# A one-layer hybrid encoder step: last output tile in halves, third norm's rows earlier, attention's filler pieces laid out anew

## The chip, the core and the metric

The kernel runs on one core of a Trainium2 chip. The metric is the device time of one execution in microseconds (us). A core has five engines that run side by side and meet at semaphores: PE (matrix products, with its weight loads listed as PEld), DVE (vector), ACT (activations), POOL (general) and SP (here it only issues DMAs).

## The reference

576 token rows (512 of a prompt, 64 of a sample that also sees 256 cached positions) go through one layer, width 1024. With h = RMSNorm(x), one projection feeds 8 heads of forgetting attention (FoX: causal, with sums of log forget gates added to the logits) and 8 heads of latent attention (MLA: low-rank queries and keys, a rotary part). Their two outputs are normalised, joined and projected (`w_o`); then comes a 4-head attention to 256 memory rows, then the feed-forward block of hidden width 2816, and a final norm:

```
x = x + mixed @ w_o
x = x + o @ w_mo                                   # o: attention of RMSNorm(x) to the memory
hf = rms_norm(x, g_ffn)                            # the third norm
x = x + (silu(hf @ w_gate) * (hf @ w_up)) @ w_down
y = rms_norm(x, g_final)
```

New keys, values, gates and latents are outputs too. All is float32.

## The kernel before, in words

**Layout.** Channels lie on the 128 partitions and the 576 tokens in the free dimension, in 8 channel tiles; `x_low` and `x_high` are the token halves 0:288 and 288:576. A float32 product is made of three products of parts: each operand is split into a high part (ACT) and a low rest (POOL or DVE), and `product` (L450 to L454) issues high x high, low x high, high x low. PSUM has eight banks; "pair p" is banks 2p and 2p+1, a token half in each.

**Weights** come in blocks: SP loads one, ACT makes the high part (`split`), POOL the low part (`rest`).

**Queries and keys of FoX.** Before the attention loop PE computes queries and keys of head pairs 0 and 1 as four whole blocks (`full`, the loop behind the value projection). DVE writes them to `qt` and `kt`; `query_dup` and `key_dup` (DVE), `query_hi` and `key_hi` (ACT), `query_lo` and `key_lo` (POOL) make the parts that the scores use. Pairs 2 and 3 are computed inside the loop.

**The attention loop** runs over ticks `s`. Tick s belongs to head s//5 and query tile s%5 (FoX heads are ticks 0 to 39, MLA heads 40 to 79). In a tick PE computes the scores of tick s, one *filler* chunk, and the transposes of tick s-2; at s%5 == 3 also `values` of an earlier head. DVE takes the maxima and evicts the last filler and half of the transposes, ACT takes the exponentials and the other half. Scores of tick s wait for the exponential of tick s-2. Filler chunks sit at ticks written out by hand: `QK_AT` (queries and keys of FoX, one token half, 24 matmuls), `UQ_AT` (MLA queries), `KP_AT` and `V_AT` (MLA keys, values), `RB_AT` (the reciprocals of a head pair's sums, spread over rows; POOL builds its source `rb` at `RB_BUILD`), `FC_AT` and `FR_AT` (norm of the FoX output: column sums, then rows; ACT takes a square root two ticks behind `FC_AT`), `WO_AT` (first half of `w_o`). `HIGH_AT`, `LOW_AT`, `REST_AT`, `SPLIT_AT`, `KR_AT` and the tables of `query_*`, `key_*` say at which tick ACT, DVE and POOL do the rest. The finished output of FoX head pair 0 first goes to a tile of its own, `olof0`, and is copied by DVE to `olof` behind tick 18 (L1712, semaphore `s_omove`), since `olof` shares its place with the low part of h; POOL's first `rb` waits for that copy.

**The third norm and the first gate and up blocks.** PE computes the gate and up products of the first two hidden tiles in full (blocks c = 0 to 3, 48 matmuls each), with column sums for the norm behind c = 0 (`columns`, L470) and the row spread (`spread`, L478) behind c = 2. The other 20 hidden tiles use seven half-size products (`seven`) of sums of weights (`weight_sums`, `op_rest`, `op_high`, `op_low`) and sums of inputs (`t_sum`, `t_high`, `t_rest`). DVE's order is: the four `t_sum`, the norm's rows, gate of tile 0, `weight_sums` of the first step, and so on; the seventh product of a step waits for DVE's `gate_low` of the step behind it (L1938).

**The end.** The down projection has 8 output tiles in three blocks each; in every block PE does both token halves. DVE multiplies by the norm's rows (L2010), adds to x (L2012), ACT squares, DVE adds to `sqacc` (L2017). Behind the last tile come column sums (L470), a square root (ACT), a reciprocal (L2019), the row spread (L478), eight multiplications of 576 columns (L2022), and eight stores.

Of the kernel before, what the change touches and what calls it, by code (L numbers as in the profile page):

```python
# [14 lines left out]
D = 1024  # L15
TP, TS = 512, 64
T = TP + TS
# [46 lines left out]
def nth(tick):  # L64
# [4 lines left out]
FILLER_END = {15: QK_AT[1], 16: QK_AT[3], 17: QK_AT[5], 18: QK_AT[7], 19: UQ_AT[1] + 1, 20: V_AT[0][6], 21: UQ_AT[3] + 1, 22: UQ_AT[5] + 1, 23: V_AT[1][6],  # L69
# [9 lines left out]
    0, 1, 6, 11, 21, 31, 36, (56, 80), 66, 71, 76, 78)  # L79

# [6 lines left out]
def build(nc, i_, o_, cum_dram):  # L87
# [38 lines left out]
    olof0, _ = place("olof0", [128, T], F32, c)  # L126
# [37 lines left out]
    vbase = c  # L164
    va, _ = place("va", [128, 2, 7, 4, 64], F32, vbase + 14336)
# [55 lines left out]
    with ExitStack() as ctx:  # L221
# [36 lines left out]
        s_init, s_mask, s_zero, s_omove = sem("s_init"), sem("s_mask"), sem("s_zero"), sem("s_omove")  # L258
# [40 lines left out]
        s_y, s_yst = sem("s_y"), sem("s_yst")  # L299
# [132 lines left out]

        def half_a(c):

            return slice(64 * (c % 2), 64 * (c % 2) + 64)
# [11 lines left out]
        def _(pe):  # L447
# [100 lines left out]
            for i in range(4):  # L548
                if i == 0:
                    pe.wait_ge(s_kvn, 2)  # L550
                else:
                    pe.wait_ge(s_vev, (2, 4, 5)[i - 1])
                full(B_QK + i, PAIR_QK[i])
# [53 lines left out]
            def values(c):  # L607
# [3 lines left out]
                if c == 0:  # L611
                    pe.wait_ge(s_vhi, 7)
                    pe.wait_ge(s_qkev, 4)
# [23 lines left out]
            def head_part(i, bank, k0):  # L637

                b, half = B_QK + 4 + i // 2, i % 2
# [6 lines left out]
            def filler(s):  # L646
                if s + 1 in QK_AT:
                    i = QK_AT.index(s + 1)
                    bank = filler_bank(nth(s + 1))
                    pe.wait_ge(f_lo, B_QK + 4 + i // 2 + 1)  # L650
# [71 lines left out]
            for s in range(LAST):  # L722
# [7 lines left out]
                if s == 84:  # L730
# [3 lines left out]
                elif s == 86:  # L734
# [3 lines left out]
                elif s == 89:  # L738
                    pe.wait_ge(n_rc, 2)
                    spread(ps[:, 5, :], small[:, S_MRC:S_MRC + 2], range(2)).then_inc(n_row, 1)  # L740
                elif s == 90:
                    memory_keys(1)
                elif s == 92:
# [3 lines left out]
                elif s == 94:  # L747
# [160 lines left out]
            for c in range(4):  # L908
                pe.wait_ge(g_lo, c + 1)
                pe.wait_ge(r_x, 8 + (5, 6, 8, 7)[c])  # L910
                wide(c, KT, lambda k: [ffw(c, lo, KT, 128)[:, k, :] for lo in (0, 1)], x1,
                     wait_k=(lambda k: pe.wait_ge(r_lo, 8 + k + 1)) if c == 0 else None).then_inc(g_used, 1)
                if c == 0:
                    pe.wait_ge(r_acc, 7 + 7)
                    pe.wait_ge(r_x, 8 + 7)
                    columns(7, sqacc, at=HT).then_inc(n_col, 1)
                if c == 2:
                    pe.wait_ge(n_rc, 5)
# [1604 lines left out]
```

## Time and profile before

| | us |
|---|---|
| runs (3) | 893.72, 894.79, 897.13; median 894.79 |
| the profiled execution | 897.35, of which the span is 895.6 |
| PE busy | 848.6, 95% of the span |
| DVE, ACT, POOL busy | 551.0, 400.5, 365.5 |
| mean granted PE clock | 0.982 of full speed |
| DMA | 75.49 MB, mean 84 GB/s |

PE has two granted clock levels, 1.2 GHz (0.50 in the rows) and 2.4 GHz (1.00). Since PE is nearly always busy, time can only come from the stretches in which it waits, from those at the lower clock, and from the end, where nothing is left for it.

### The profile page before, as it was taken

The page shows a single profiled execution, that of the slowest core. Times are in us where ns is not written, and L with a number is a line of the kernel's source. Part 1 is how long each engine was busy: PE and PEld are TensorE (multiplying, and loading weights), DVE is VectorE, ACT ScalarE, POOL GpSimd, SP SyncE. Part 2 cuts the span into 40 slices and gives each one's busy share as a digit, 9 for nine tenths or more (in the row PEclk, how much of TensorE's full clock was granted, in tenths as well). Part 3 has the DMA queues.
Part 4 walks back from the last instruction along what each step waited for, and adds up shares of the span by engine and source line. Part 5 has one row for each costly group of instructions (what it writes and reads, how often), then busy time and mean ns, then how long its engine had stood idle before and what let it go on. Part 6 is the DMA issues. An engine that isn't in the chain of part 4 may idle for free.

```text
span 895.6 us, 16042 instructions
## 1 busy us (share of the span) xinstructions
PE 848.6 (95%) x5930; PEld 784.8 (88%) x5930; DVE 551.0 (62%) x875; ACT 400.5 (45%) x736; POOL 365.5 (41%) x212
## 2 busy tenths in 40 slices
PE   6999999899999899989899989999999999999994
PEld 6988988677887799978589989999999998999994
DVE  5256354656555854863546899999999989312213
ACT  6443454535556533444535455555555555222110
POOL 2644854634422544662129233333333335433410
PEclk9999999999999999999999999999999999999997
DMA  7332421100105323333012212222222233223102
GB/s 244 109 111 69 156 80 44 56 1 19 48 1 172 113 65 91 120 112 97 0 45 98 94 49 94 94 94 93 94 94 94 93 127 90 87 85 89 42 1 106
DMA packets 25239, 75.49 MB, mean 84 GB/s; under 512 B 2896, under 2 KB 5272, under 8 KB 25048
## 3 DMA queue, kind: packets, MB, share of 16 engines
q1 hardware_dynamic: 25184, 74.74, 26.2%
q8 instruction: 37, 0.61, 0.3%
q14 instruction: 18, 0.15, 0.1%
HBM read 68.20 MB, written 6.53 MB: 83 GB/s over the span
## 4 chain that ended last, share of the span: by engine, by line
PE 71%; DVE 6%; issue 3%; ACT 1%; POOL 0%; DVEq 0%; ACTq 0%
PE ps L452 21%; PE ps L453 20%; PE ps L454 20%; PE ps L619 3%; PE ps L603 1%; PE ps L855 1%; PE ps L470 1%; PE ps L478 1%; DVE xb L2022 1%; DVE hlo L1753 1%; DVE tl L1863 1%; PE ps L625 0%; PE ps L588 0%; PE ps L582 0%; DVE sqacc L1760 0%
## 5 line engine op out<-in xcount | busy, mean ns | idle before, releaser
L452 PE MATMUL ps<-hhi,whi 128*128 128x288 f32 x896 | 270.0, 301 | 18.8 <-DVE hlo L1455 6.6
L453 PE MATMUL ps<-hhi,wlo 128*128 128x288 f32 x896 | 266.1, 297 | 0.0
L454 PE MATMUL ps<-hlo,whi 128*128 128x288 f32 x800 | 237.8, 297 | 0.0
L2033 POOL TENSOR_TENSOR wlo<-wraw,whi 128x1024 fp32r<-128x1024 f32 (+1 forms) x48 | 115.3, 2407 | 212.2 <-ACT whi L980 203.1
L452 PEld LDWEIGHTS ps<-hhi,whi 128*128 128x128 f32 x896 | 170.3, 190 | 22.2 <-issue 10.5
L980 ACT ACTIVATE whi<-wraw 128x1024 fp32r<-128x1024 f32 (+3 forms) x138 | 114.8, 838 | 137.3 <-PE ps L454 119.8
L453 PEld LDWEIGHTS ps<-hhi,wlo 128*128 128x128 f32 x896 | 169.9, 190 | 0.1
L454 PEld LDWEIGHTS ps<-hlo,whi 128*128 128x128 f32 x800 | 151.5, 189 | 0.0
L2179 POOL TENSOR_TENSOR wlo<-wraw,whi 128x512 fp32r<-128x512 f32 x60 | 77.3, 1302 | 155.2 <-ACT whi L980 155.2
L454 PE MATMUL ps<-hidlo,whi 128*128 128x288 f32 x352 | 103.9, 295 | 0.0
L2193 POOL TENSOR_TENSOR wlo<-wraw,whi 128x1024 fp32r<-128x1024 f32 (+1 forms) x24 | 56.8, 2372 | 77.6 <-ACT whi L980 77.6
L1606 DVE TENSOR_REDUCE small<-ps 128x1 f32<-128x128 f32 (+4 forms) x80 | 39.0, 488 | 75.6 <-PE ps L588 54.5
L454 PE MATMUL ps<-tl,whi 128*128 128x288 f32 x240 | 71.4, 297 | 0.0
L452 PE MATMUL ps<-th,whi 128*128 128x288 f32 x240 | 71.0, 296 | 0.4 <-DVE wlo L1909 0.4
L453 PE MATMUL ps<-th,wlo 128*128 128x288 f32 x240 | 71.3, 297 | 0.0
L980 ACT ACTIVATE whi<-ss 128x512 fp32r<-128x512 f32 x61 | 38.4, 632 | 65.3 <-PE ps L454 37.5
L454 PEld LDWEIGHTS ps<-hidlo,whi 128*128 128x128 f32 x352 | 66.1, 188 | 0.0
L980 ACT ACTIVATE probs<-ps,small 128x128 f32<-128x128 f32 (+4 forms) x80 | 41.9, 524 | 49.4 <-DVE small L1606 48.8
L2010 DVE TENSOR_TENSOR tmp<-ps,rstd 128x576 f32<-128x576 f32 x8 | 6.1, 758 | 88.8 <-PE ps L454 88.8
L452 PE MATMUL ps<-hidhi,whi 128*128 128x288 f32 x192 | 56.8, 296 | 2.1 <-DVE hidlo L1992 2.1
L453 PE MATMUL ps<-hidhi,wlo 128*128 128x288 f32 x192 | 56.8, 296 | 0.0
L452 PEld LDWEIGHTS ps<-th,whi 128*128 128x128 f32 x240 | 45.2, 188 | 0.6 <-DVE wlo L1909 0.6
(277 smaller groups left out, 1870.8 us busy)
## 6 DMA issues: line engine op xcount, KB each, us to landing
wraw<-w_ff SPq DMA_DIRECT2D x44, 512.0 KB, 4.1
wraw<-w_front SPq DMA_DIRECT2D x41, 512.0 KB, 3.6
wraw<-w_down SPq DMA_DIRECT2D x16, 512.0 KB, 3.6
wraw<-w_down SPq DMA_DIRECT2D x8, 384.0 KB, 3.3
wraw<-w_front SPq DMA_DIRECT2D x7, 384.0 KB, 3.6
xs<-x_t SPq DMA_DIRECT2D x8, 288.0 KB, 6.1
xa<-x_t SPq DMA_DIRECT2D x8, 288.0 KB, 5.1
out_y<-xb SPq DMA_DIRECT2D x8, 288.0 KB, 2.3
```

What stands on the lines that cost most here:

```text
L452: nc.tensor.matmul(out, lh, rh, start=start, stop=False)
L453: nc.tensor.matmul(out, ll, rh, start=False, stop=False)
L454: return nc.tensor.matmul(out, lh, rl, start=False, stop=stop)
L470: mm = nc.tensor.matmul(ps[:, bank, at + tt:at + tt + 1], source[:, 128 * tt:128 * tt + 128], ones[:, 0:1], start=True, stop=True)
L478: mm = nc.tensor.transpose(out[:, at:at + n], col[0:n, tt:tt + 1].to_broadcast([n, 128]), ident[0:n, 0:n])
L603: mm = nc.tensor.transpose(ps[:, 2 + s % 2, 128 * kb:128 * kb + n], probs[0:n, P_AT[u] + 128 * kb:P_AT[u] + 128 * kb + 128], ident[0:n, 0:n])
L619: mm = nc.tensor.matmul(ps[0:64, 4, 128 * kb:512], va[:, g, kb, h, :], pt[:, 512 * kb:512 * kb + 512 - 128 * kb], start=kb == 0, stop=kb == 3)
L980: return nc.scalar.activation(out, src, func, **kw)
L1606: v.tensor_reduce(nmax, ps[0:n, s % 2, 0:w], AX, ALU.max, negate=True).then_inc(s_mx, 1)
L2033: g.tensor_tensor(wlo[:, b % 3, 0:n], wraw[:, b % 2, 0:n], f(whi[:, b % 3, 0:n]), ALU.subtract).then_inc(f_lo, 1)
L2179: g.tensor_tensor(w_operand(1, j), src, f(w_operand(0, j)), ALU.subtract).then_inc(g_lo, 1)
L2193: g.tensor_tensor(ffw(n, 1, 1, w)[:, 0, :], (wraw2, wraw)[n % 4 // 2][:, n % 2, 0:w], f(ffw(n, 0, 1, w)[:, 0, :]), ALU.subtract).then_inc( ...
```

## The change: what it does

Three parts. (1) The last output tile of the down projection is computed one token half after the other. Column sums, square root, reciprocal and rows of the final norm are made for each half by itself, in tiles of 96 tokens, those of the first half between the products of the second; outputs are written and stored in halves (16 stores). A square root without use is put ahead, at tile 6. (2) The third norm's rows are spread in the middle of block c = 1; DVE does the first step's `weight_sums` and the gate of tile 0 ahead of all four `t_sum`; ACT and DVE orders follow; PE waits for DVE's copy of the rows (`n_rs`) ahead of c = 2. (3) The key block of FoX pair 1 moves from ahead of the loop into ticks 1 and 3; all filler ticks are laid out anew, with one tick more; FoX outputs get a tile `fo` of their own, so the copy and `s_omove` go.

```diff
-LAST = 95
-QK_AT = (1, 3, 5, 7, 12, 14, 16, 18)
-UQ_AT = (24, 34, 43, 45, 49, 56, 60, 69)
-KP_AT = (30, 40, 51, 62)
-V_AT = ((28, 29, 32, 33, 38, 39, 42), (54, 55, 58, 59, 64, 65, 66))
-RB_AT = (22, 26, 36, 47, 67, 73, 79, 85)
-FC_AT = 53
-FR_AT = 71
-WO_AT = (75, 77, 81, 83, 87, 89, 91, 93)
+LAST = 96
+QK_AT = (1, 3, 5, 7, 10, 12, 15, 17, 20, 22)
+UQ_AT = (25, 34, 36, 46, 50, 56, 64, 70)
+KP_AT = (30, 40, 54, 60)
+V_AT = ((27, 32, 33, 42, 43, 44, 45), (52, 53, 58, 59, 62, 63, 66))
+RB_AT = (23, 28, 38, 48, 68, 74, 78, 86)
+FC_AT = 67
+FR_AT = 72
+WO_AT = (76, 80, 82, 84, 88, 90, 92, 94)
...
-            for i in range(4):
+            for i in range(3):
...
                 full(B_QK + i, PAIR_QK[i])
...
+                if c == 2:
+                    pe.wait_ge(n_rs, 5)
+                for k in range(KT):
+                    if c == 0:
+                        pe.wait_ge(r_lo, 8 + k + 1)
+                    if c == 1 and k == 4:
+                        pe.wait_ge(n_rc, 5)
+                        for tt in range(TT):
+                            bank, at = (4 + tt, HT) if tt < 4 else (7, HT + 128)
+                            mm = spread(ps[:, bank, at:512], small[:, S_RCC:S_RCC + 5], range(tt, tt + 1))
+                        mm.then_inc(n_row, 1)
...
+            for half in range(2):
+                cc = slice(half * HT, half * HT + HT)
+                for c in range(3):
...
+                        if half == 1 and t == 6:
+                            last_columns(0)
+                        elif half == 1 and t == 13:
+                            last_rows(0)
...
+            last_columns(1)
+            last_rows(1)
...
-            HIGH_AT = (25, 30, 39, 50, 70, 76, 82, 88)
+            HIGH_AT = (26, 31, 41, 51, 71, 77, 81, 89)
...
             first = (0, None)
+            early_silu(0)
+            op_high(0, first)
+            op_high(1, first)
+            op_high(2, first)
+            op_high(3, first)
             t_high(0)
             t_high(1)
             t_high(2)
-            op_high(0, first)
-            op_high(1, first)
-            early_silu(0)
-            op_high(2, first)
-            op_high(3, first)
...
-            LOW_AT = (26, 31, 40, 51, 71, 77, 83, 89)
+            LOW_AT = (27, 32, 42, 52, 72, 78, 82, 90)
...
-                if s == QK_AT[7] + 1:
-                    dve.wait_ge(s_o, 2)
-                    v.tensor_copy(olof[:, 0, :], olof0[:, :]).then_inc(s_omove, 1)
...
             first = (0, None)
+            dve.wait_ge(n_sd, 5)
+            v.reciprocal(small[:, S_RCC:S_RCC + 5], small[:, S_COL:S_COL + 5]).then_inc(n_rc, 1)
+            weight_sums(first)
+            dve.wait_ge(n_row, 5)
...
             early_gate(0)
-            weight_sums(first)
             early_hidden(0)
+            t_sum(1, hf[:, 0:4, x_high], hf[:, 0:4, x_low])
...
+            dve.wait_ge(d_half, 1)
+            residual(KT - 1, KT - 1, x_low, ps[:, 6, 0:HT], lambda a: a)
+            squares(KT - 1, x_low)
+            reciprocals(0)
+            outputs(0, range(4))
+            dve.wait_ge(g_used, 4 + 7 * NW + 3 * KT)
+            residual(KT - 1, KT, x_high, ps[:, 7, 0:HT], lambda a: a)
+            outputs(0, range(4, 6))
+            squares(KT, x_high)
+            outputs(0, range(6, 8))
+            reciprocals(1)
+            outputs(1, range(8))
...
-            RB_BUILD = (20, 24, 31, 41, 51, 70, 75, 82)
-            KR_AT = (26, 31, 36, 41)
+            RB_BUILD = (12, 26, 31, 41, 51, 70, 76, 82)
+            KR_AT = (27, 32, 37, 42)
...
-            sp.wait_ge(s_pv, 12)
+            sp.wait_ge(s_olo, 4)
...
-            for j in range(KT):
-                sp.wait_ge(s_y, j + 1)
-                sp.dma_start(o_["y"][:, T * j:T * j + T], xb[:, j, :]).then_inc(s_yst, 16)
+            for n in range(2 * KT):
+                j, at = n % KT, n // KT * HT
+                sp.wait_ge(s_y, n + 1)
+                sp.dma_start(o_["y"][:, T * j + at:T * j + at + HT], xb[:, j, at:at + HT]).then_inc(s_yst, 16)
```

The ticks of `query_*` of heads 4 to 7 go from 6, 11, 16 or 17, 21 to 9, 10, 19, 20, those of `key_*` from 0 or 2 up to 22 to 5, 6, 14, 15, 24, 25; SP's loads in the loop follow the same order.

## Rows read from the trace of the kernel before

**Rows 1.** Waits of PE: line <- what ended them: us in total, times, longest

```profile
PE ps L452 <- DVE tmp L1938: 2.7, 1, 2.7
PE ps L619 <- issue: 2.3, 2, 2.0
```

**Rows 2.** Windows: length; busy PE, PEld, DVE, ACT, POOL; clock, DMA share, GB/s

```profile
160.60:164.00 3.40, 1.14 (x8) 0.78 (x8) 3.31 (x7) 2.23 (x6) 2.96 (x3) 0.99 0.80 220
164.00:167.40 3.40, 3.40 (x10) 1.95 (x11) 3.34 (x6) 2.48 (x6) 3.32 (x2) 0.50 0.44 147
188.80:191.30 2.50, 0.54 (x3) 0.24 (x3) 2.46 (x6) 0.67 (x2) 1.08 (x1) 0.99 0.00 0
...
306.80:309.00 2.20, 0.90 (x6) 0.60 (x6) 2.20 (x5) 2.20 (x6) 0.54 (x1) 1.00 0.45 151
...
510.00:522.40 12.40, 8.53 (x61) 7.89 (x60) 11.71 (x19) 6.38 (x11) 2.52 (x2) 1.00 0.25 85
522.40:525.80 3.40, 3.40 (x16) 3.40 (x15) 3.37 (x8) 1.12 (x2) 1.82 (x1) 0.50 0.21 28
871.00:880.10 9.10, 9.07 (x69) 8.84 (x67) 0.00 (x0) 0.00 (x0) 0.00 (x0) 1.00 0.01 2
```

**Rows 3.** Timeline of the end, DVE, ACT and PE: start us, us, instruction, idle before

```profile
880.11 0.76 DVE L2010 TENSOR_TENSOR tmp<-ps,rstd 128x576 f32<-128x576 f32 x1 [14.48 <-PE ps L454]
...
886.82 5.89 DVE L2022 SCALAR_TENSOR_TENSOR xb<-xb,gains,ps 128x576 f32<-128x576 f32 x8 [1.51 <-PE ps L478]
...
881.70 0.68 ACT L980 ACTIVATE tmp<-xb 128x576 f32<-128x576 f32 x1 [16.91 <-DVE xb L2012]
...
884.83 0.27 ACT L980 ACTIVATE small<-ps,small 128x5 f32<-128x5 f32 x1 [1.15 <-PE ps L470]
...
883.28 1.51 PE L470 MATMUL ps<-ones,sqacc 128*128 128x1 f32 x10 [3.21 <-DVE sqacc L2017]
885.37 1.42 PE L478 MATMUL ps<-ident,small 128*128 128x128 f32 x5 [0.58 <-DVE small L2019]
```

**Rows 4.** Timeline of PE at the third norm: column sums and row spread between products

```profile
485.97 1.17 PE L470 MATMUL ps<-ones,sqacc 128*128 128x1 f32 x10
...
499.87 0.80 PE L478 MATMUL ps<-ident,small 128*128 128x128 f32 x5
```

**Rows 5.** Groups by shape, DVE, 512 to 745: busy us, mean ns, idle before

```profile
L1938 DVE TENSOR_TENSOR tmp<-ps,pp 128x288 f32<-128x288 f32 x20 | 8.9, 446 | 0.4 <-PE ps L454 0.4
```

**Rows 6.** Timeline of DVE and ACT around the third norm

```profile
491.37 3.54 DVE L1859 TENSOR_TENSOR tf<-hf 128x1152 f32<-128x1152 f32 x1 [5.70 <-POOL hf L2160]
495.02 1.36 DVE L1859 TENSOR_TENSOR tf<-hf,tf 128x1152 f32<-128x1152 f32 x1
...
500.70 0.69 DVE L1872 COPY rstd<-ps 128x512 f32<-128x512 f32 x1 [1.73 <-PE ps L478]
...
488.74 0.27 ACT L980 ACTIVATE small<-ps,small 128x5 f32<-128x5 f32 x1
```

**Rows 7.** Timeline of DVE and ACT ahead of the attention loop, PE's first score

```profile
104.73 3.13 DVE L1566 CAST q<-qt 64x576 fp32r<-64x576 f32 x2
...
107.22 1.28 ACT L980 ACT_TABLE_LOAD   x1
...
110.13 0.22 PE L582 MATMUL ps<-k,q 128*128 128x128 f32 x1
```

**Rows 8.** Timeline of DVE around tick 32

```profile
187.08 1.55 DVE L1721 SCALAR_TENSOR_TENSOR hlo<-olof,gains,hhi 128x576 fp32r<-128x576 f32 x1
```

**Rows 9.** Timeline of ACT at ticks 55 and 56, of POOL and PE ahead of tick 75

```profile
247.63 1.28 ACT L980 ACT_TABLE_LOAD   x1
...
249.24 1.28 ACT L980 ACT_TABLE_LOAD   x1
...
288.55 2.37 POOL L2033 TENSOR_TENSOR wlo<-wraw,whi 128x1024 fp32r<-128x1024 f32 x1 [6.57 <-ACT whi L980]
...
292.34 0.33 PE L452 MATMUL ps<-k,q 128*128 128x128 f32 x1 [0.59 <-POOL q L2108]
```

More of the change, by code:

```diff
@@ L164, in build @@
     vbase = c
+    fo, _ = place("fo", [128, 4, T], F32, vbase)
     va, _ = place("va", [128, 2, 7, 4, 64], F32, vbase + 14336)
@@ L431, in mturned, with out_of @@
             return ps[:, s % 2, 0:256].rearrange("p (b q) -> p b q", q=128)[:, :, 0:tok(s % 5)]
+        def out_of(j):
+            return fo[:, j, :] if j < 4 else olof[:, j, :]
         def half_a(c):
@@ L637, in head_part @@
             def head_part(i, bank, k0):
[L639 removed]
+                b, half = B_QK + 3 + i // 2, i % 2
                 c = slice(half * HT, half * HT + HT)
@@ L910, in _ @@
                 pe.wait_ge(r_x, 8 + (5, 6, 8, 7)[c])
-                wide(c, KT, lambda k: [ffw(c, lo, KT, 128)[:, k, :] for lo in (0, 1)], x1,
-                     wait_k=(lambda k: pe.wait_ge(r_lo, 8 + k + 1)) if c == 0 else None).then_inc(g_used, 1)
+                if c == 2:
[11 more added lines that the diff above has]
+                        cc = slice(half * HT, half * HT + HT)
+                        mm = product(ps[:, 2 * c + half, 0:HT], [ffw(c, lo, KT, 128)[:, k, :] for lo in (0, 1)],
+                                     [t[:, k, cc] for t in x1], k == 0, k == KT - 1)
+                mm.then_inc(g_used, 1)
                 if c == 0:
                     pe.wait_ge(r_acc, 7 + 7)
[L915 to L918, printed above, removed]
-                    for tt in range(TT):
-                        mm = spread(ps[:, tt, HT:512], small[:, S_RCC:S_RCC + 5], range(tt, tt + 1))
-                    mm.then_inc(n_row, 1)
+                    pe.wait_ge(r_x, 8 + 8)
+                    columns(7, sqacc, at=HT + 192).then_inc(n_col, 1)
             def seven(p):
@@ L950, in _ @@
             seven((NW - 1, None))
-            for n, (m, c) in enumerate(DOWN):
+            for n, (m, c) in enumerate(DOWN[:-3]):
                 kn = DOWN_K[c]
@@ L1620, in joined @@
                 r = slice(64 * (c % 2), 64 * (c % 2) + 64)
-                v.tensor_copy(olof0[r, :] if c < 2 else olof[r, c // 2, :], flat[0:64, 4 * 512:4 * 512 + T]).then_inc(s_o, 1)
+                v.tensor_copy(out_of(c // 2)[r, :], flat[0:64, 4 * 512:4 * 512 + T]).then_inc(s_o, 1)
             def evicted(s):
@@ new lines, in squares @@
+            def squares(count, cols):
+                dve.wait_ge(r_x, 16 + count + 1)
+                dve.wait_ge(r_sq, 16 + count + 1)
+                dve.wait_ge(s_init, 3)
+                need(dve, r_acc, 14 + count)
+                v.tensor_tensor(sqacc[:, cols], sqacc[:, cols], tmp2[:, 0, cols], ALU.add).then_inc(r_acc, 1)
+            for m in range(KT - 1):
+                dve.wait_ge(g_used, 4 + 7 * NW + (5 + m if m < 2 else 3 * m + 3))
+                residual(m, m, slice(0, T), two(2 * (m % 2) + 1), halves)
+                squares(m, slice(0, T))
@@ new lines, in reciprocals, with outputs @@
+            def reciprocals(half):
+                dve.wait_ge(n_sd, 6 + half)
+                v.reciprocal(small[0:96, S_LRC + 3 * half:S_LRC + 3 * half + 3], small[0:96, S_LSD + 3 * half:S_LSD + 3 * half + 3])\
+                    .then_inc(n_rc, 1)
+            def outputs(half, tiles):
+                cc = slice(half * HT, half * HT + HT)
+                dve.wait_ge(n_row, 6 + half)
+                for j in tiles:
+                    v.scalar_tensor_tensor(xb[:, j, cc], xb[:, j, cc], gain(G_FIN, j), ps[:, half, 0:HT], ALU.mult, ALU.mult)\
+                        .then_inc(s_y, 1)
```

220 lines of the change are left out of this document (114 added, 106 removed).

## The prediction, as it was made

> **What bounds the kernel now.** The waits of PE come first, because PE is busy through 95% of the span: only its waits, its slow stretches and the end can give time. The list shows 2.7 us before the seventh product of the first half-size step (released by L1938) and 2.0 us before a `values` [rows 1]. The windows are read second, for the idle time around each wait and for the clock behind it. At 160.6 to 164.0 PE idles 3.40 - 1.14 = 2.26 us, at 188.8 to 191.3 1.96 us, at 510 to 522.4 12.40 - 8.53 = 3.87 us; behind each stand 3.4 us at clock 0.50, the lower of the two levels, in which half of the work is lost, 1.7 us. At 306.8 PE idles 1.30 us and nothing slow follows [rows 2]. So a short wait costs itself and one near 2 us costs 1.7 us more. The timeline of the end is read third: PE's last product ends at about 880.1, and all that follows, 895.6 - 880.1 = 15.5 us, is a chain with one engine active at a time [rows 3].
>
> **The end: -3.9 us.** Removed is the chain of 576 columns: 6.7 us from L2010 to the first output multiplication (886.82 - 880.11), 5.9 us of multiplications, and 2.9 us from the last of them to the end of the span [rows 3]. Added to PE's stream, between the products of the second half, are the first half's three column sums and three transposes: 6/10 of 1.17 and 3/5 of 0.80 us, 1.2 us [rows 4]. They wait for nothing: seven k of three matmuls lie between the half's end and its columns (21 x 0.131 = 2.8 us; 9.07 us for 69 of them [rows 2]), DVE and ACT need 4 x 0.45. Behind the last product: two operations of 288 columns, 0.9 us by the nearest shape [rows 5]; ACT's square beside two output multiplications (0.9), the addition (0.45), column sums 6/10 of 1.51, square root 0.3, reciprocal 0.2, spread 3/5 of 1.42 [rows 3], together 4.6 us to the first output of the second half. Eight outputs cost half of 5.89, say 3.1 us, and the way out 2.7. That makes 1.2 + 4.6 + 3.1 + 2.7 = 11.6 instead of 15.5. The bounds are -5.3 (no insertion cost, outputs wholly hidden by the way of the stores) and -2 (the inserted pieces drain PE's pipeline, stores of half rows as dear as whole ones: eight more of them). Sixteen stores cost SP issue time, but half of them leave during PE's second half. Hoisting the square root's table costs nothing and gives nothing: its load lay beside the addition and column sums.
> The Trainium skill speaks against half-size stores (DMA: Bandwidth & Descriptors, section Bandwidth): batch to 1 MiB, small transfers run far below peak. Between its figures for 64 KB and 1 MB (138 and 341 GB/s) a store of 144 KB would move at an estimated 200 GB/s, and the last eight would end some 3 us later than their outputs. The rows speak for a smaller price: stores of 288 KB keep step with a multiplication each 5.89 / 8 = 0.74 us and end 2.9 us behind the last [rows 3].
>
> **The third norm and the sums: -1.4 us, and -1.7 us of slow clock.** DVE is in arrears here: it works through 11.71 of 12.40 us while PE idles 3.87 [rows 2]. Removed from DVE's road to L1938: its start moves from 491.4 to 489.1, when ACT's root is done (2.3 us); the first `t_sum`, held by POOL's subtraction for 3.54 - 1.36 = 2.2 us, comes later; the wait for the rows, 1.7 us, goes because the spread now lies at c = 1 beside the weight sums [rows 6]; small holds of about 2.5 us are replaced. Sum 8.7. Added: the weight sums read two SBUF operands and are now held by POOL's two 2.4 us subtractions of blocks 2 and 3 (0.4 and 2.3 us); the gate's way through ACT and back, 0.75 us, with nothing between; the `t_sum` held by POOL's two first low parts, up to 2.5; other holds 1.2. Sum 7.2 to 7.4. Net -1.4; bounds -3.5 (holds fall between operations) and +0.5. The new wait: PE stands before c = 2 until DVE has copied the rows. DVE is through with reciprocal (0.2), four sums (0.7 each, as the copy of 512 columns [rows 6]), holds of 2.7 and two copies (0.9) at 495.7; PE is through with columns, c = 1 and spread at 485.97 + 1.17 + 48 x 0.131 + 0.80 = 494.2 [rows 4]: 1.5 us. Behind it queue c = 2, c = 3 and the first seven products, which wait for DVE anyway, so it only shifts idle time from the place of L1938, where 1.5 of the 3.87 us stay. Two waits of 1.5 are nearest to the 1.30 that drew no slow stretch, so I take the 1.7 us as regained; the bounds are 0 and 1.7.
>
> **The attention pieces: -2.2 us in five terms.** PE's work is the same; only waits change.
> *Start, +1.5.* The loop begins 48 matmuls (6.4 us) earlier. Tick 2 needs the first exponential. DVE's two `query_dup` hold it until 107.9, ACT's table load until 108.5, so the exponential is there at 109.0; PE's first score moves from 110.1 to 103.7, and scores and chunks of ticks 0 and 1 (24 matmuls) last until 107.6 [rows 7]. Bounds 0 and +3.2 (with a slow stretch).
> *Ticks 19 to 23, -3.5.* Here stood 2.26 us of idle and 1.7 of slow clock: no filler at ticks 19 to 21, an olof copy in DVE's queue, and `rb` behind it [rows 2]. Now chunks lie at 20 and 22, `rb` is built at tick 12, the copy is gone. I keep 0.5 us for DVE's crowd at ticks 24 and 25, where key copies, the join and an eviction meet. Bounds -4.0 and -1.
> *Tick 33, -2.4.* `values` waited 1.96 us for a transposed half that stood behind DVE's low part, 1.55 us [rows 8]. That part is now behind it, but ACT's high part and square moved by one tick too and delay the key parts that DVE waits for; I get 1.3 us of wait in place of 1.96, and, nearest to the 1.30 row, no slow stretch. Bounds -3.7 and 0.
> *Tick 75, +3.5.* The column sums of the FoX norm go from tick 53 to 67, and so do ACT's two table switches: 249.24 + 1.28 - 247.63 = 2.9 us without an exponential [rows 9]. At tick 55 they lay free; at 69 the high part of tile 4, the memory squares, a weight split and an MLA query's high part follow, and POOL's weight rest (2.37 us) and that query's low part wait for them. PE waited 0.59 us for it [rows 9]. By counting ACT through from tick 69, the low part is ready at 295.2 and PE, 1.15 us later by the chunks moved in, at 292.9: 2.35 us, 1.8 more, and with the nearest row at 1.96 a slow stretch of 1.7. Bounds 0 and +4.
> *Ticks 79 to 81, -1.3.* The `rb` eviction that PE waited for stands one tick earlier, with a full tick of scores between [rows 2]; bounds -1.5 and 0.
> The 16 loads and copies that SP passes keep two to five ticks of room; SP's new wait for `s_olo` 4 (tick 52) is over before its next one, the scores of tick 64. POOL's `rb` at tick 76 stands behind the memory additions of tick 75 and is needed at 78: hidden, 1 us if not.
>
> **Sum.** -3.9 - 3.1 - 2.2 = -9.2. The profiled execution took 897.35, 2.56 above the median; against itself it gives 888.15, against the median 894.79 - 9.2 = 885.6.
>
> **The rivals.**
> *A, ACT absorbs the switches at tick 69.* For it: at ticks 55 to 57 the same 2.9 us left PE without any wait. Against it: ACT's queue behind tick 69 is fuller. Then +3.5 is 0 and the time 882.1.
> *B, the new ticks are a wash,* each wait that goes being replaced by one elsewhere, since the attention is a loop of PE, DVE, ACT, PE; and the slow stretch behind the sums stays. Then -3.9 - 1.4 = -5.3, 889.5. For it speaks that three of my five terms rest on waits reckoned to tenths.
> *C, slower.* From tick 69 to 83 DVE makes the memory's low parts between all else. If ACT's lateness brings them beside POOL's work, each of the eight can be held for nearly one POOL operation (2.37 us [rows 9]), say 2.0, 16 us in all, on an engine that already leaves no room (2.20 of 2.20 busy at 306.8 [rows 2]): 885.6 + 16 = 901.6. The whole is slower once more than 9.2 us of it lie on PE's path. Against it: PE idled only 1.30 there.
> *D, a table switch that costs more than its load.* If ACT stood for another load's length, 1.28 us, at each of the two switches, tick 75 would be later by 2.6: 888.2. The rows speak against it: both loads and the root between them end 2.9 us after the first began [rows 9]. The Trainium skill (ScalarE: Activation LUTs, What ACT_TABLE_LOAD costs) gives a drain of 1.38 us beside the load of 1.28.
>
> **Numbers.** Forecast as reckoned, 0.48 (by itself 881 to 890); A 0.20; B 0.22; C 0.05; D 0.05. A measurement of this kernel tells about 0.5%, 4.5 us, from no change: faster means below 890.3. That takes 0.95 of the forecast, all of A, 0.6 of B, most of D: 0.83. Slower, above 899.3, is C, or several bounds at once: 0.05. The rest, 0.12, is the same. The range 879 to 892 takes in A with the end at its best, and B with a wait at each new place; it leaves out C.
>
> **What would show it.** From PE's last product to the end about 10.4 us, with column sums and transposes of the first half between products, and no wait before them. A wait of 1 to 2 us before c = 2, released by DVE's copy of the rows, one near 1.5 before L1938's product, and clock 1.00 behind both. A wait near 1.5 at tick 2, none for `rb` at tick 23, under 1.5 at tick 33, over 2 before tick 75 for POOL's low part. I am wrong if the span between the last product and the end stays above 13.5, if the attention (110 to 324) does not shorten with the 6.4 us added to it reckoned in, or if the clock is 0.50 behind c = 2.

## The result, and the profile after

| | before | changed |
|---|---|---|
| median of the runs | 896.49 us (893.72 to 900.39) | 889.49 us (888.49 to 892.39) |
| ratio, 95% interval | | 0.9923 [0.9895, 0.995] |
| profiled execution, its span | 897.35, 895.6 | 888.72, 886.9 |
| mean granted PE clock | 0.982 | 0.987 |

The changed kernel is faster by 7.0 us (4.5 to 9.4 by the interval). The forecast was 9.2 less. The two profiled executions differ by 8.6. The same kernel measured twice more beside the experiments gave 0.9914 [0.9889, 0.9939] and 0.9904 [0.9878, 0.9931].

The lines of the helpers have moved: `product` is L457 to L459, `columns` L475, `spread` L483, `values` L624; DVE's L1938 is L1984, L1668 is L1717, and POOL's L2108 is L2176. L987 and L994 are the new column sums and transposes of the end, one token half each.

The waits of PE, changed kernel (line <- what ended them: us in total, times, longest; answers to [rows 1]):

```profile
PE ps L624 <- issue: 3.3, 3, 1.6
...
PE ps L457 <- DVE fo L1717: 2.1, 3, 1.6
PE ps L457 <- POOL q L2176: 2.0, 1, 2.0
...
PE ps L587 <- ACT probs L1026: 1.3, 1, 1.3
PE ps L457 <- DVE tmp L1984: 0.8, 1, 0.8
PE ps L457 <- DVE rstd L1953: 0.8, 1, 0.8
```

The 2.7 us before the seventh product have become 0.8, and 0.8 more stand at the new wait for the rows. But the attention has not fewer waits than before: `values` waits three times, POOL's low part of a query is awaited for 2.0 us where it was 0.59, and a wait of 1.6 us for DVE's `fo` (an `rb` eviction) is new.

Windows behind the longest waits, changed kernel (length; busy PE, PEld, DVE, ACT, POOL; clock, DMA share, GB/s; answers to [rows 2]):

```profile
172.40:175.80 3.40, 3.40 (x24) 2.88 (x24) 2.91 (x7) 3.23 (x9) 2.01 (x2) 1.00 0.02 5
188.70:192.10 3.40, 3.40 (x21) 2.22 (x22) 1.50 (x3) 0.95 (x3) 0.00 (x0) 1.00 0.00 0
...
291.00:294.40 3.40, 3.40 (x26) 3.06 (x26) 2.77 (x6) 1.35 (x6) 3.32 (x2) 1.00 0.06 18
...
516.50:519.90 3.40, 3.02 (x23) 2.79 (x22) 3.40 (x8) 1.89 (x4) 1.83 (x1) 1.00 0.02 5
736.50:739.90 3.40, 3.40 (x16) 3.40 (x17) 3.40 (x4) 3.40 (x7) 2.20 (x1) 0.56 0.00 0
```

None of the first four is at the lower level, not even the one behind the 1.98 us wait at 291. The one at 736.5 is (0.56: its first tenths are still at the higher level). So are three stretches ahead of the third norm, at 385, 430 and 447 us, where the profile of before has two, at 440 and 451. Whether this belongs to the kernel or to the execution is a question for the experiments.

Timeline of the end, changed kernel, PE, DVE and ACT (start us, us, instruction, idle before; answers to [rows 3]):

```profile
869.63 0.59 PE L987 MATMUL ps<-ones,sqacc 128*96 128x1 f32 x6
...
872.96 0.41 PE L994 MATMUL ps<-ident,small 96*128 96x96 f32 x3
...
876.31 0.29 PE L459 MATMUL ps<-hidlo,whi 128*128 128x288 f32 x1
876.64 0.46 DVE L2055 TENSOR_TENSOR tmp<-ps,rstd 128x288 f32<-128x288 f32 x1 [1.44 <-PE ps L459]
877.13 0.46 DVE L2057 TENSOR_TENSOR xb<-xb,tmp 128x288 f32<-128x288 f32 x1
...
878.86 0.67 PE L987 MATMUL ps<-ones,sqacc 128*96 128x1 f32 x6 [2.26 <-DVE sqacc L2064]
...
880.09 0.59 PE L994 MATMUL ps<-ident,small 96*128 96x96 f32 x3 [0.56 <-DVE small L2073]
880.72 3.49 DVE L2080 SCALAR_TENSOR_TENSOR xb<-xb,gains,ps 128x288 f32<-128x288 f32 x8 [0.69 <-PE ps L994]
```

PE's last product ends at 876.6 and the span at 886.9: 10.3 us, where 15.5 stood. The first half's sums and transposes lie between products (869.63, 872.96) and nothing waits for them.

Timelines at the third norm, changed kernel, DVE (first fence) and PE (second; answer to [rows 4, 6]):

```profile
488.86 2.88 DVE L1940 TENSOR_TENSOR ss<-wraw 128x512 f32<-128x512 f32 x1
491.67 0.68 DVE L1952 COPY rstd<-ps 128x512 f32<-128x512 f32 x1
```

```profile
487.66 0.80 PE L483 MATMUL ps<-ident,small 128*128 128x128 f32 x5
492.62 0.37 PE L457 MATMUL ps<-hhi,whi 128*128 128x288 f32 x1 [0.77 <-DVE rstd L1953]
...
516.11 0.37 PE L457 MATMUL ps<-hhi,whi 128*128 128x288 f32 x1 [0.80 <-DVE tmp L1984]
```

The last weight sum is held (2.88 us where the same shape takes 0.69 unheld); PE waits 0.77 for the rows behind it. The seventh product starts 516.11 - 483.33 = 32.8 us behind the column sums instead of 521.17 - 485.97 = 35.2.

### The profile page after: what moved, and what is told of

Read it like the earlier page. It is cut to its first block, busy times and chain, and to the rows that moved or that the text cites. A ratio compares the mean times of both kernels' runs of the same rounds, so it can differ in the third digit from the quotient of the medians.

```text
span 886.9 us, 16075 instructions
## 1 busy us (share of the span) xinstructions
PE 844.6 (95%) x5933; PEld 783.5 (88%) x5933; DVE 551.8 (62%) x887; ACT 401.3 (45%) x739; POOL 365.8 (41%) x212
## 4 chain that ended last, share of the span: by engine, by line
PE 82%; DVE 7%; issue 4%; ACT 3%; POOL 3%; DMA 1%; SPq 0%; DVEq 0%; ACTq 0%
PE ps L457 24%; PE ps L459 23%; PE ps L458 23%; PE ps L624 4%; PE ps L608 2%; POOL hf L2228 1%; PE ps L860 1%; ACT whi L1026 1%; PE ps L587 1%; PE ps L475 1%; POOL wlo L2105 1%; DMA wraw<-w_front 1%; DVE tf L1905 1%; PE ps L588 1%; PE ps L483 1%
## 5 line engine op out<-in xcount | busy, mean ns | idle before, releaser
L457 PE MATMUL ps<-hhi,whi 128*128 128x288 f32 x896 | 270.3, 302 | 15.6 <-DVE hlo L1510 6.6
L459 PE MATMUL ps<-hlo,whi 128*128 128x288 f32 x800 | 237.6, 297 | 0.0
L457 PEld LDWEIGHTS ps<-hhi,whi 128*128 128x128 f32 x896 | 170.3, 190 | 19.0 <-issue 10.4
L459 PEld LDWEIGHTS ps<-hlo,whi 128*128 128x128 f32 x800 | 151.4, 189 | 0.0
L459 PE MATMUL ps<-hidlo,whi 128*128 128x288 f32 x352 | 104.6, 297 | 0.0
L459 PE MATMUL ps<-tl,whi 128*128 128x288 f32 x240 | 71.4, 297 | 0.0
L457 PE MATMUL ps<-th,whi 128*128 128x288 f32 x240 | 70.9, 295 | 0.0
L459 PEld LDWEIGHTS ps<-hidlo,whi 128*128 128x128 f32 x352 | 66.8, 190 | 0.0
L457 PE MATMUL ps<-hidhi,whi 128*128 128x288 f32 x192 | 57.6, 300 | 2.1 <-DVE hidlo L2038 2.1
L2055 DVE TENSOR_TENSOR tmp<-ps,rstd 128x576 f32<-128x576 f32 (+1 forms) x9 | 6.2, 690 | 85.2 <-PE ps L459 85.2
L457 PEld LDWEIGHTS ps<-th,whi 128*128 128x128 f32 x240 | 45.2, 188 | 0.0
```

The costliest lines, as they stand in the source:

```text
L457: nc.tensor.matmul(out, lh, rh, start=start, stop=False)
L459: return nc.tensor.matmul(out, lh, rl, start=False, stop=stop)
```

## The experiments

Each kernel was timed beside runs of the kernel before on the same chip; ratios are to those. To compare stretches of different executions, the time lost to the lower clock is taken off where that is said: busy PE times (1 - clock), summed over windows of half a microsecond. A full slow stretch comes to 1.7 us.

### Each part alone

**Part 1 alone** (the kernel before with the last output tile in halves):

```diff
-            for n, (m, c) in enumerate(DOWN):
+            for n, (m, c) in enumerate(DOWN[:-3]):
...
+            last_columns(1)
+            last_rows(1)
```

> The kernel before with part 1 alone (last output tile in halves). My theory: the span between PE's last product and its own end falls from 15.5 to 10.5 us, 1.0 us of column sums and transposes of the first half is added between products, so -4.0 us, ratio 0.9955; the third norm and the attention keep their waits (2.7 us before the seventh product, 2.0 before a values group). Rival B (everything in the attention is a wash and part 1 carries most of the gain): the ratio is 0.992 or lower. Rival, small stores: if a store of 144 KB were no cheaper than one of 288 KB, the last store would end 3 us later and the end would be above 13 us. A slow stretch behind a wait of 2 us is expected at 161 to 164 and 191 again, if it belongs to the place; if it varies between executions, at least one of the three stretches of before (164, 191, 522) is missing or another wait near 2 us has one.

Measured: 892.51 us, ratio 0.9939 [0.9916, 0.9963], -5.5 us: the expected 0.9955 lies inside the interval, the rival's 0.992 just inside its other end, so the runs alone don't part the two. From the last product to the end 887.76 - 877.55 = 10.2 us. The way from the wait at 737 us to the last product takes 140.15 us; in the two profiles without part 1 that also have the slow stretch behind that wait (parts 2 and 3 alone, below) it takes 139.3: the inserted pieces cost 0.85. Together -5.3 + 0.85 = -4.4. The end is at 10.2 and not above 13, as it would be if a store of half the size were no cheaper. Its windows, as above:

```profile
163.00:166.40 3.40, 3.40 (x21) 1.94 (x20) 3.37 (x5) 3.13 (x7) 3.32 (x2) 1.00 0.36 135
188.50:191.90 3.40, 3.40 (x10) 1.65 (x9) 0.38 (x2) 0.94 (x3) 0.00 (x0) 0.53 0.00 0
...
737.60:741.00 3.40, 3.40 (x18) 3.40 (x18) 3.40 (x4) 3.40 (x7) 2.37 (x1) 0.59 0.00 0
```

The attention is that of before and waits to 0.02 us as there (0.93 and 1.31 at 160.4 and 162.7, 1.95 at 188.0). Yet the first of its slow stretches, the one at 164.0 in [rows 2], is missing, and one stands at 737 where the first profile of before has none.

**Part 2 alone** (third norm and order of the sums):

```diff
+                if c == 2:
+                    pe.wait_ge(n_rs, 5)
...
+            weight_sums(first)
+            dve.wait_ge(n_row, 5)
...
             early_gate(0)
-            weight_sums(first)
```

> The kernel before with part 2 alone (third norm's rows and the first sums ahead of the input sums). My theory: -1.4 us of shifted work, and -1.7 us if the slow stretch behind the sums goes: ratio 0.9965 with it, 0.9985 without. In the profile a wait of 0.8 us before c = 2, one of 0.8 before the seventh product in place of 2.7, and 33 us instead of 35 from the column sums to the seventh product. Rival: the two new waits make up for the old one, ratio 1.000, and the distance from column sums to seventh product stays at 35 us.

Measured: 896.35 us, ratio 0.997 [0.9947, 0.9992], -2.7 us. It takes 519.15 - 485.88 = 33.3 us from the column sums to the seventh product, with waits of 1.28 before c = 2, 0.90 before the seventh product and 0.61 for the step behind. Its window behind the seventh product:

```profile
519.20:522.60 3.40, 3.35 (x24) 3.12 (x24) 3.37 (x8) 2.22 (x5) 1.84 (x1) 1.00 0.02 5
```

No slow stretch. The rival of two waits in place of one fails.

**Part 3 alone** (the attention):

```diff
-            for i in range(4):
+            for i in range(3):
...
-QK_AT = (1, 3, 5, 7, 12, 14, 16, 18)
+QK_AT = (1, 3, 5, 7, 10, 12, 15, 17, 20, 22)
...
-                        dve.wait_ge(s_omove, 1)
```

> The kernel before with part 3 alone (key block of pair 1 in the loop, filler ticks laid out anew, a tile of their own for the FoX outputs). My theory: the last values group of the attention starts 2.2 us (forecast) to 4.1 us (the two profiled executions) earlier: ratio 0.9955 to 0.9975. Waits as in the profile of the changed kernel: 1.3 at tick 2, 1.6 at tick 26 for DVE's eviction, 1.6 at tick 33, 1.2 at tick 43, 2.0 before tick 75 for POOL's low part. Rival B (a wash): ratio 1.000, last values group at 315 as before. If the slow stretches vary between executions, the gain in this profile differs from 4.1 us by 1.7 or 3.4 while the waits stay.

Measured: 897.68 us, ratio 0.999 [0.9972, 1.0009]: no difference that can be told. The last `values` group begins at 312.2 us instead of 315.7, as the theory had it. But that mark doesn't tell the two apart: in the other three profiles with the old attention it lies at 312.8 to 314.1, and other pieces follow it in the new layout. All waits came as in the changed kernel, to 0.02 us (1.28, 1.62, 1.57, 1.19, 1.97). Its window behind the wait for POOL's low part:

```profile
290.10:293.50 3.40, 3.40 (x16) 3.07 (x17) 2.09 (x5) 0.85 (x3) 3.32 (x2) 0.52 0.11 39
```

The same wait of 1.97 us drew a slow stretch here and none in the first profile of the changed kernel.

**Parts 1 and 2, the attention of before,** with the changed kernel beside it:

> The kernel before with parts 1 and 2, without the new attention layout. If the new layout is a wash (0.7 us more work and waits, fewer slow stretches), this is as fast as the changed kernel within 1.5 us: ratio 0.991 to 0.993. If the layout brought the 2.2 us of the forecast or more, it is 2 to 4 us slower than the changed kernel. The slow stretch behind the wait before the seventh product is gone (wait under 1), that behind the 1.96 wait at 189 us is there.

> The changed kernel a third time, as the measure for the two beside it: waits as in its first two profiles, from first score to the memory keys 247.5 us without the lost clock; its slow stretches may lie elsewhere. From PE's last product to the end 10.5 us.

Measured: 891.03 us, ratio 0.9917 [0.989, 0.9945]; changed kernel 890.71, 0.9904 [0.9878, 0.9931]. The new layout is worth 0.3 us by the medians and 1.2 by the ratios, less than the intervals can tell from nothing. The stretch behind the 1.94 wait at 188 us is there (clock 0.50), that behind the seventh product is gone.

### The waits of the new layout

**The changed kernel again,** unaltered:

> The changed kernel once more, as the measure for the three beside it. Every wait of PE as in its first profile to 0.1 us (1.62 at tick 26, 1.57 at tick 33, 1.98 before tick 75). If slow stretches belong to places, they lie at 385, 430, 447 and 737 us as there; if they vary, at least one differs. From first score to the memory keys 247.6 us after subtraction of the lost clock.

Measured: 889.78 us, 0.9914. Every wait came back (1.27, 1.62, 1.57, 1.19, 1.98), and from the first score to the memory keys (here the product near 353 us that waits 0.61 us for DVE's `kmf`) it took 247.4 us without the lost clock. But its windows are these:

```profile
172.50:175.90 3.40, 3.40 (x19) 2.81 (x19) 2.29 (x6) 2.99 (x7) 2.20 (x2) 0.68 0.02 5
...
292.60:296.00 3.40, 3.40 (x18) 3.17 (x18) 2.82 (x6) 1.32 (x6) 3.32 (x2) 0.59 0.12 45
```

Two slow stretches at places where the first profile of the same kernel has none: waits belong to the kernel, slow stretches partly to the execution.

**Tick 75.** The chain there in the changed kernel, ACT, POOL and PE, one fence each:

```profile
278.55 1.28 ACT L1026 ACT_TABLE_LOAD   x1
```

```profile
287.19 2.37 POOL L2105 TENSOR_TENSOR wlo<-wraw,whi 128x1024 fp32r<-128x1024 f32 x1 [8.78 <-ACT whi L1026]
289.52 1.40 POOL L2176 TENSOR_TENSOR q<-qf,q 128x576 fp32r<-128x576 f32 x1
```

```profile
290.98 0.33 PE L457 MATMUL ps<-k,q 128*128 128x128 f32 x1 [1.98 <-POOL q L2176]
```

Two edits take this chain apart. The first changes POOL's order:

```diff
-            REST_AT = {4: 17, 8: 18, 13: 19, 18: 20, 23: 21, 36: 22, 46: 23, 48: 24, 59: 25, 67: 26, 72: 27, 82: 28, 86: 29,
+            REST_AT = {4: 17, 8: 18, 13: 19, 18: 20, 23: 21, 36: 22, 46: 23, 48: 24, 59: 25, 67: 26, 74: 27, 82: 28, 86: 29,
```

> The changed kernel with POOL's low part of weight block 27 two ticks later (74 instead of 72), behind the low part of the MLA query that tick 75 waits for. POOL then starts the query's part at 285.6 instead of 289.5. My theory (the wait before tick 75 is POOL's queue, made late by ACT): the wait of 1.98 us there goes to under 0.3, nothing takes its place, since block 27 is not read before tick 85: -2 us against the changed kernel. Rival (the loop stands for ACT anyway after the table loads): the wait at tick 75 is replaced by waits of together 1.5 us or more at ticks 72 to 80 for exponentials or for DVE's evictions.

Measured: 888.87 us, ratio 0.9882 [0.9855, 0.9909]. POOL, which had been idle, starts the query's part as soon as ACT's part is there:

```profile
286.79 1.41 POOL L2176 TENSOR_TENSOR q<-qf,q 128x576 fp32r<-128x576 f32 x1 [7.27 <-ACT q L1026]
288.29 2.37 POOL L2105 TENSOR_TENSOR wlo<-wraw,whi 128x1024 fp32r<-128x1024 f32 x1
```

The wait at tick 75 is gone; one of 0.40 us behind it, for an eviction, is new. First score to memory keys is 245.9 in place of 247.5 us without the lost clock.

The second takes away ACT's table loads, and with them the square root of the FoX norm, so this kernel computes something else and serves for its times alone:

```diff
-                    deviation(small[:, S_COL:S_COL + 5], small[:, S_COL:S_COL + 5], 512).then_inc(s_lsd, 1)
+                    activation(small[:, S_COL:S_COL + 5], small[:, S_COL:S_COL + 5], scale=1.0 / 512).then_inc(s_lsd, 1)
```

> The changed kernel with a plain scaling in place of ACT's square root at tick 69, so that neither table load is made there; the root of the FoX norm is left out of the computation. My theory of the wait before tick 75: ACT's two loads (2.56 us) make the query's high part, the weight split and so POOL's low part late. Then POOL's part starts 2.6 us earlier, at 286.9, the wait of 1.98 goes to under 0.1 and the kernel is faster by 2.0 us. Rival: POOL's order alone (weight rest ahead of the query) makes the wait; then the low part comes at most 1 us earlier and 1 us or more of wait stays.

Measured: 888.13 us, ratio 0.9897 [0.9871, 0.9923]. The wait falls from 1.98 to 1.27 us only: POOL's low part starts at 287.81 instead of 289.52, of which 1.0 us is that the first score of this execution came earlier; 0.7 is left, not 2.6. ACT had 1.7 us of idle time between the removed loads and the query's part. The rival expectation is the right one: POOL's order alone removes the whole wait (above), leaving out the loads takes 0.7 us of it.

**Tick 26.** DVE, POOL and PE in the changed kernel:

```profile
169.51 2.34 DVE L1631 CAST k<-kt 64x832 fp32r<-64x832 f32 x1
171.88 0.29 DVE L1656 TENSOR_REDUCE small<-ps 128x1 f32<-128x128 f32 x1
172.09 0.21 DVE L1717 TENSOR_TENSOR fo<-fo,ps 128x64 f32<-128x64 f32 x1
172.33 0.59 DVE L1631 CAST k<-kt 64x832 fp32r<-64x832 f32 x1
```

```profile
169.45 1.94 POOL L2140 TENSOR_TENSOR k<-kt,k 64x832 fp32r<-64x832 f32 x1 [1.25 <-ACT k L1026]
```

```profile
172.35 0.40 PE L457 MATMUL ps<-cqhi,whi 128*128 128x288 f32 x1 [1.62 <-DVE fo L1717]
```

One copy takes 2.34 us beside POOL's subtraction, the next, beside nothing, 0.59. The eviction that frees PE's bank stands behind the held one.

```diff
-            KEY_DUP_AT = {5: 2, 6: 3, 14: 4, 15: 5, 24: 6, 25: 7}
+            KEY_DUP_AT = {5: 2, 6: 3, 14: 4, 15: 5, 25: 6, 26: 7}
```

> The changed kernel with DVE's key copies of heads 6 and 7 one tick later (25 and 26), behind the eviction of the second rb chunk. Theory: the wait of 1.62 at tick 26 is the first copy held 1.75 us (2.34 instead of 0.59 us) by POOL's low part of the same keys, which runs beside it; with the copy behind the eviction, the wait goes to under 0.3 and the kernel is 1.4 us faster. Rival: the copy is held as long at its new place and the wait turns up at tick 27 or at the next exponential; then the sum of waits between 165 and 185 us stays within 0.5 us of 2.1.

Measured: 887.98 us, ratio 0.9896 [0.9871, 0.992]; changed kernel 0.9914. The wait at tick 26 is gone and none took its place; first score to memory keys 246.0 us. The copy is still held, 1.81 us, but PE waits for nothing behind it. By the times alone none of the three kernels with one edit (this one and the two at tick 75) can be told from the changed one, their intervals overlap with its own; the waits in the traces tell them apart.

**All repaired,** the two edits at ticks 24 and 74 and ACT's and DVE's part of FoX output tiles 1 and 2 two ticks later:

```diff
-            HIGH_AT = (26, 31, 41, 51, 71, 77, 81, 89)
+            HIGH_AT = (26, 33, 43, 51, 71, 77, 81, 89)
...
-            LOW_AT = (27, 32, 42, 52, 72, 78, 82, 90)
+            LOW_AT = (27, 34, 44, 52, 72, 78, 82, 90)
```

> The changed kernel with four pieces moved: POOL's rest of block 27 to tick 74, the key copies one tick later, and the high parts and squares of FoX output tiles 1 and 2 from ticks 31 and 41 to 33 and 43 (their low parts from 32 and 42 to 34 and 44), so that ACT makes the MLA key parts first and DVE's transposed half, which the values wait for, comes earlier. Expected: wait at tick 26 under 0.3, at tick 33 0.4 in place of 1.57, at tick 43 0.3 in place of 1.20, before tick 75 under 0.4; together 4.5 to 5 us less wait, and the time 884.5 to 886, ratio to before 0.987. Rival: waits move on to the next tick, because the loop of PE, DVE, ACT and PE is full there; then the sum of waits between 165 and 300 us stays above 5 us and the gain under 2 us.

Measured: 884.73 us, ratio 0.9859 [0.9831, 0.9887]; the changed kernel beside it 889.78, 5.0 us more. PE's waits of more than 0.15 us between 165 and 304 us sum to 3.5 us, in the first profile of the changed kernel to 7.9: at tick 33 0.61, at tick 43 0.54, none at 26 and 75, 0.40 new at two places. First score to memory keys 243.4 in place of 247.5 us. Its interval lies wholly below that of the changed kernel beside it (0.9889 to 0.9939), if only just.

### The stores

```diff
-            for n in range(2 * KT):
-                j, at = n % KT, n // KT * HT
-                sp.wait_ge(s_y, n + 1)
-                sp.dma_start(o_["y"][:, T * j + at:T * j + at + HT], xb[:, j, at:at + HT]).then_inc(s_yst, 16)
+            for j in range(KT):
+                sp.wait_ge(s_y, KT + j + 1)
+                sp.dma_start(o_["y"][:, T * j:T * j + T], xb[:, j, :]).then_inc(s_yst, 16)
```

> The changed kernel with eight whole stores of 288 KB, each issued when the second half of its tile is written, in place of sixteen of 144 KB. My theory: half of the bytes then no longer leave during PE's second half, and the stores can't keep step with outputs of 0.44 us: at the 0.74 us each that the stores of the kernel before kept, the last lands 8 x 0.74 + 2.3 us behind the first output, about 2.4 us later than now; PE's last product to end 12.5 to 13 us in place of 10.5. Rival (small stores are dear): with half as many issues of twice the size the end stays at 10.5 or gets shorter.

Measured: 891.74 us, ratio 0.9927 [0.9901, 0.9953]; changed kernel 0.9904. By the times the two can't be told apart. In the trace the last product and the end are 892.6 - 880.0 = 12.6 us apart in place of 10.2. The DMA issues of this kernel and then of the changed one (KB each, median us to landing):

```profile
out_y<-xb SPq DMA_DIRECT2D x8, 288.0 KB, 3.1
```

```profile
out_y<-xb SPq DMA_DIRECT2D x16, 144.0 KB, 1.9
```

Windows of the end, three of the changed kernel (up to its last product, up to the first output of the second half, stores under way) and one of this kernel (stores under way); the last number is GB/s:

```profile
860.00:876.60 16.60, 16.60 (x128) 16.37 (x126) 4.09 (x9) 1.21 (x3) 0.00 (x0) 1.00 0.10 35
876.60:880.70 4.10, 1.26 (x9) 0.89 (x9) 3.15 (x8) 0.70 (x2) 0.00 (x0) 0.95 0.35 125
882.50:886.00 3.50, 0.00 (x0) 0.00 (x0) 1.71 (x5) 0.00 (x0) 0.00 (x0) 0.50 0.89 299
```

```profile
886.00:891.50 5.50, 0.00 (x0) 0.00 (x0) 1.64 (x4) 0.00 (x0) 0.00 (x0) 0.50 1.00 387
```

The small stores are the slower ones, 299 GB/s against 387. They win because they start early: 16.6 x 35 = 0.58 MB, a quarter of the 2.36 MB of output, has moved when the last product ends, and 0.51 MB more by the first output of the second half. No run has half-size stores that all start late, so how much the size alone costs in time stays open.

## Why the prediction was right, and where it was off

The direction, the order of the parts and the end were right. The time is 3.9 us above the forecast. The kernel before had a median of 896.5 beside the changed one and 894.8 in the runs the forecast started from, which is 1.7 of them; the other 2.2 are the terms. It lies inside the range of 879 to 892. That it came so near rests on the end and on the norm; the attention, a quarter of the forecast, brought nothing that can be told. What the thirteen profiles of this case give for each stretch (in brackets how many profiles; differences of the means, in the last row of the middle values; "memory keys" is the wait for `kmf`; the second row leaves out the kernels that repair the new attention):

| stretch | old form | new form | difference |
|---|---|---|---|
| start to first score, without lost clock | 108.4 to 109.0 (4) | 101.5 to 102.9 (9) | -6.5 |
| first score to memory keys, without lost clock | 240.6 (4) | 247.4 to 247.7 (5) | +6.9 |
| memory keys to third norm's column sums | 130.4 to 133.5 (4) | 131.7 to 135.3 (9) | +1.1 |
| third norm's column sums to the wait at 737 | 255.7 to 256.2 (3) | 253.1 to 253.8 (10) | -2.4 |
| that wait to PE's last product | 139.3 (2) | 140.1 to 140.3 (10) | +0.85 |
| last product to end | 15.5 to 16.3 (3) | 10.2 to 10.5 (9) | -5.3 |

**The end: forecast -3.9, found -4.4.** The step from the last product to the end was reckoned at 10.4 us and is 10.2 to 10.5: 4.1 to the first output (forecast 4.6), 3.49 of outputs (3.1), 2.7 way out (2.7). The insertion costs 0.85 and not 1.2. The smaller price for half-size stores, read from [rows 3], came out: the last eight end 2.7 us behind their last output. The estimate of 200 GB/s from the Trainium skill's figures (DMA: Bandwidth & Descriptors, section Bandwidth) was too low: they moved at 299. That smaller transfers are slower, as the Trainium skill's rule has it, holds here with 299 against 387. Storing in whole tiles costs 2.4 us of the end. The gain comes from the early start of the stores, which the prediction named only in passing and too large: a quarter of the output, not half, leaves during PE's second half, since DVE writes only four of the first half's eight outputs before PE's last product ends.

**Third norm and sums: forecast -3.1 with the clock, found -2.4.** The two new waits came out at 0.8 to 1.4 before c = 2 and 0.8 to 0.9 before the seventh product (1.5 forecast for each). But PE waits 0.6 us more for DVE's L2008, one step on, which was not reckoned. Without the lost clock the stretch is 0.7 us shorter (forecast 1.4); the slow stretch is the other 1.7, as forecast. Of the two terms it is the surer one: behind the 2.66 wait the lower level stood in 3 of 3 profiles with the old order, in none of 10 with the new.

**The rule for slow stretches.** That "one near 2 us costs 1.7 us more" was read from three waits that had such a stretch. The same profile held others as long that had none, of 2.27, 1.82 and 2.12 us. The lines of the first and the last of them, and the windows behind these two:

```profile
PE ps L452 <- DVE hlo L1753: 3.9, 2, 2.3
...
PE ps L452 <- DVE hidlo L1992: 2.1, 1, 2.1
```

```profile
387.50:390.90 3.40, 2.68 (x18) 2.44 (x18) 3.40 (x3) 1.87 (x2) 2.40 (x1) 1.00 0.00 0
742.20:745.60 3.40, 3.40 (x25) 3.40 (x26) 3.40 (x4) 3.40 (x7) 2.17 (x1) 1.00 0.00 0
```

So the 1.7 us should have gone into the sum with a chance for each place, not as a price. Four of the terms carry it: it held for the norm, at tick 33 and mostly at tick 75, and not at ticks 19 to 23.

**The attention: forecast -2.2, found about 0.** This is the step that failed, and by the prediction's own sign, taken up to the memory keys: with the 6.4 us added to it the old stretch would take 240.6 + 6.4 = 247.0 us, and the new one takes 247.5. The waits over 0.15 us in PE's timeline sum to 9.2 us in the new attention and to 7.6 in the old. Of the five terms:
- Start: 1.28 us, forecast 1.5.
- Ticks 19 to 23: the waits there are gone as forecast, but "I keep 0.5 us for DVE's crowd at ticks 24 and 25" was short. That crowd costs 0.24 + 1.62, since DVE's key copy is held 1.75 us by POOL's subtraction of the same keys. I had priced such holds at the third norm and not here.
- Tick 33: 1.57, forecast 1.3, and no slow stretch (8 of 8 profiles with this wait), as taken.
- Tick 75: 1.98, forecast 2.35; the stretch of 1.7 stood behind it in 5 of 6 profiles, though not in the first. The size is right, the cause only in part: by the two experiments ACT's table loads make 0.7 us of it, and POOL's order alone can remove it all. The prediction had POOL's weight rest in the chain, but put the lateness down to ACT.
- Ticks 79 to 81: 0.49 remains where 1.6 stood (1.28, 0.17 and 0.18), so -1.1 of the -1.3.
- Not in the sum at all: tick 43 (1.20, before 0.32) and the one at 261 us (0.54). Tick 43 has the same pattern as tick 33, ACT's high part and square ahead of the key parts, and moving both out of the way brought 1.0 and 0.7 us; I reckoned the one that had a long wait before and not its twin.
- "Here stood 2.26 us of idle and 1.7 of slow clock": the waits stood in all four profiles with the old attention, the slow stretch in one. So of the -3.5 only some 2.2 (an estimate: 2.26 + 1.7 / 4 - 0.5) could be had on average.

That leaves 6.9 - 6.5 = +0.4 us of work and waits and a slow clock that is nearly the same on both sides: old 1.25 stretches on average (5 in 4 profiles), new 5 of 6 and 2 of 7, about 1.1. (The waits alone grew by 1.6; the other 1.2 went because PE is busy that much less in the two stretches, for a reason that no run shows.)

Behind the attention, where PE's code is the same in both kernels, lies a stretch that the forecast left out: from the memory keys to the third norm's column sums. The lost clock there is 1.7 to 5.0 us with the old attention (mean 3.4, 4 profiles) and 4.7 to 8.2 with the new (mean 5.6, 9 profiles). Half of that is made good: where a slow stretch stands behind the 2.26 us wait for DVE's `hlo`, the next wait for it is 0.1 to 0.8 us, elsewhere 1.63. All told the stretch is 1.1 us longer. A slow stretch begins between 381 and 393 us in 9 of 9 profiles with the new attention and in 1 of 4 with the old; whether the layout brings it or chance does, no run decides.

The sum of what was found, -4.4 - 2.4 + 0.2 = -6.6, stands inside the intervals of the three measurements (they begin at -4.5, -5.5 and -6.2). With the 1.1 us just named it is -5.5, at the edge of the second and outside the third. The profiled executions of the second and third were the slowest of their six, so slow stretches counted in profiles are likely too many. The single parts measured -5.5, -2.7 and -0.9. The 1 to 3 us between these sums and the measured 7.0 to 8.6 are below what the runs resolve, and stay open.

**The rivals.** B (the attention is a wash) is what came true in its main point, against its second one: the slow stretch behind the sums is gone. That its 889.5 is the measured median to a tenth is luck; from the 896.5 measured beside the changed kernel its -5.3 makes 891.2. A does not hold, since ACT did not absorb the switches, though little depended on them. C did not come up: behind tick 75 PE waits for nothing over 0.5 us in the loop. D: both loads and the root again take 281.45 - 278.55 = 2.9 us, so a switch costs no second load's length; the drain of 1.38 us that the Trainium skill states (ScalarE: Activation LUTs, What ACT_TABLE_LOAD costs) is not seen between the rows.

## What to carry to other kernels

Before a piece is moved, list for both queues, DVE and POOL, what runs side by side at the new place: a DVE copy beside a POOL subtraction took 2.34 us instead of 0.59, and behind it stood the eviction that PE needed. When one place of a repeated pattern is repaired, count its twins, which share the order and not the wait. The end of a kernel that cannot be shortened can be halved: work split so that the first half's tail, and its first stores, lie under the second half's products. Before a slow stretch is priced, look in the same trace for waits as long that have none.

## What the hardware showed that was not expected

Most waits repeat to 0.05 us between executions (in the attention all of them, the one before c = 2 not: 0.8 to 1.4); the slow stretches behind them do not. In profiles that had the wait, the lower of PE's two levels followed the 2.66 us wait in 3 of 3, the 2.1 us at 737 in 12 of 13, the 1.95 at 188 (old) in 4 of 4, the 1.98 at 291 (new) in 5 of 6, the 1.62 at 172 in 2 of 7, the pair of 0.93 and 1.31 with work between in 1 of 4, and the 1.57 at 189 in none of 8. Slow stretches can also cost next to nothing: from the memory keys to the column sums the changed kernel's first profile took 131.7 us with three of them, parts 1 and 2 without part 3 took 131.8 with two, since DVE catches up while PE is at the lower level, and the 1.63 us wait for it shrinks to 0.12. The one profile of before that lacks the stretch at 737 and the one of the changed kernel that lacks it at 291 were just those the first comparison used. With 1.7 us each, one profile against another can mislead by 3 us, more than parts 2 and 3 are worth; the single runs of the changed kernel spread over 4 us, and in the first six the mean granted clock is 0.988 in the fastest and 0.983 in the slowest, which fits the same cause.
